# A gated SSD branch turned before its gate: from token-major to channel-major gating in a two-layer decoder trunk

## The chip, the cores and the metric

The kernel runs on one NeuronCore of a Trainium2 chip, as one launch. The metric is the device time of the launch in microseconds (us). Three runs of the kernel before took 1465.75, 1467.34 and 1467.36 us; the median is 1467.34 us. The profile was taken from a further execution.

## What is computed

The model is a trunk of two layers over 1024 prompt tokens, 16 meta tokens ahead of them and 8 sample tokens (one new token each, with a state of its own). Layer 0 is gated linear attention (GLA), layer 1 a Mamba-2 scan (SSD). Everything is fp32 in and out. What matters here is the end of layer 1's mixer (shapes: `l` tokens, 2048 channels in 4 groups of 512):

```python
S, y = segmented_scan(ssd_chunk_step, S0g, (x, dt, dt * A, Bm, Cm), seg_lens)
y = y + d_skip.astype(f32).reshape(SSD_GROUPS, SSD_HPG)[..., None] * x
y = y.reshape(bsz, l, SSD_DINNER) * jax.nn.silu(z)
yg = y.reshape(bsz, l, SSD_GROUPS, SSD_DINNER // SSD_GROUPS)
yg = yg * lax.rsqrt(jnp.mean(yg * yg, axis=-1, keepdims=True) + NORM_EPS)
y = yg.reshape(bsz, l, SSD_DINNER) * w_norm.astype(f32)
out = y.astype(h.dtype) @ w_out
```

So for each token and each group of 512 channels: the scan's output y is multiplied by a gate z, the mean of the squares of the product gives one factor per token, and the product goes through the output weights. The factor is applied after the output product.

## The kernel before, in words

**Tiling.** Tokens are cut into 9 steps: step s = 0 holds the 24 sample and meta tokens, steps 1 to 8 hold 128 prompt tokens each. Channels of a layer are cut into 4 units u. Steps 0 to 4 are group G = 0, steps 5 to 8 group G = 1. An event is one pair (u, s); layer 1 has 36, in the order G, u, s (`EVENTS`, line 54). Layer 1's outputs are handled in almost the same order (`OUTPUTS`, line 57), with step 0 of a unit behind its steps 1 to 4.

**Two kinds of work on TensorE.** The input projection ("pieces", line 1515) is cut into parts of 6 matmuls, with the weights and activations split into a high and a low fp32r half. The products with the output weights are at line 879: 24 matmuls of 512 columns for a step of 128 tokens. Between them stand the small fp32 matmuls of the scans.

**One order for all engines.** The class `Plan` makes one list of tasks. Every engine walks through this same list and issues what is its own, so each engine's instructions stand in the list's order and a wait at the head of an engine's queue holds up all that is behind it. A step of layer 1 is written by hand as a list of places (`ssd`, `first`, `step`, `close`, lines 231 to 247); a number beside a name says which event it serves (0: this one, 1: the next, -1: the one before). `("fill", x)` puts parts of the input projection there; x is a share, and the planner scales it so that a unit's pieces come out even. The pieces of the input projection run out in unit u = 2 of group 1: from there to the end the fills are empty. That stretch is the tail.

**An event of layer 1 before the change**, with its lines:

- scan: TensorE reads the state (2621), makes the state's update in the bank SU (2624) and the step's own part (2631). VectorE updates the state (2653, 2656) and sums the output y, 128 tokens on partitions x 512 channels, in SBUF (2645, 2660, 2664, 2668). The last of them counts up `y_summed`.
- gates: TensorE turns z, which was loaded with channels on partitions, into tokens on partitions, in bank SU (4 transposes, 2711; in the tail in another bank).
- norm: VectorE multiplies y by it (2725).
- inputs of the next event: TensorE turns x and B and multiplies B by C (2457 to 2459); ScalarE and VectorE prepare them (2466, 2485 to 2499).
- products of the event before: 24 matmuls (879); ScalarE (u = 0) or VectorE (line 2243, else) adds the two halves to the accumulator.
- turn: TensorE turns the gated y back to channels on partitions (4 transposes, 2741, bank SU). ScalarE copies it as the high half (2750), VectorE subtracts for the low half (2759). ScalarE squares the gated y and sums along the row (2734); GpSimd makes the mean and the root (2406, 2409).
- The next scan on TensorE waits until bank SU is read (`banks_free`, line 2563: `yt_lo`).

For step 0 the answers of the samples are turned as well (2695, with z at 2711) and added (2719). GpSimd also issues the loads and stores of the samples' states (2379, 2389). z comes from DRAM in the same task as the chunk of x, B, C, two events ahead (line 2333), on SP's queue; that queue also carries the weights (853, 857) and the stores of the pieces (1691).

Layer 0 has the same need and fills it in another way: its squares are made with channels on partitions and summed over partitions by matmuls against a column of ones (2164, 16 for a step), which ScalarE copies out (2176).

## Time and profile before

| | |
|---|---|
| runs shown | 1465.75, 1467.34, 1467.36 us; median 1467.34 us |
| profiled execution, its own time | 1462.42 us |
| its span | 1460.4 us |
| TensorE busy | 1399.5 us (96%) |
| VectorE busy | 1146.5 us (79%) |
| ScalarE busy | 832.8 us (57%) |
| GpSimd busy | 231.9 us (16%) |
| TensorE clock granted, mean | 0.991 of full speed |

PE is TensorE, PEld its weight loads, DVE VectorE, ACT ScalarE, POOL GpSimd, SPq SyncE's queue. Matmuls are pipelined: the duration of one includes its drain, so several in a row are closer together than they are long. Layer 1's events run from about 680 us to the end.

### The profile page before, as it was taken

The numbers are of one execution on the slowest core, as the hardware profiler recorded it, in microseconds if no ns is written. First come the engines' busy times: TensorE is split into PE (matmuls) and PEld (weight loads), VectorE is DVE, ScalarE is ACT, GpSimd is POOL, SyncE is SP. The second block draws the span as 40 slices with busy tenths as digits, with TensorE's granted clock in tenths as the row PEclk, the third lists the DMA queues.
The fourth block names the chain that finished last, engine by engine and source line by source line (L and its number), as shares of the span: only waits on it lengthen the run. The fifth ranks groups of instructions, "written<-read, shape, count | busy, mean of one in ns | idle before, by whom it ended". The sixth has DMA issues, their size and how long they took to land. (4 is left out here: it accounts for less than half of the span.)

```text
span 1460.4 us, 32342 instructions
## 1 busy us (share of the span) xinstructions
PE 1399.5 (96%) x12082; PEld 1173.2 (80%) x12082; DVE 1146.5 (79%) x2495; ACT 832.8 (57%) x1877; POOL 231.9 (16%) x429
## 2 busy tenths in 40 slices
PE   6999998999999899998999999989999999999987
PEld 6999897778888789997978888867777777777765
DVE  5566678676878987889796998986889688588786
ACT  5755645485556555556666664654656365555553
POOL 6010201011322100121211220120012110000003
PEclk9999999999999999998999999999999999999999
DMA  7485747266585435376844844852675674554463
GB/s 214 141 254 156 213 116 237 85 195 178 136 253 156 132 120 166 101 187 192 259 137 157 252 129 139 235 150 64 202 231 146 192 198 121 176 166 150 135 195 66
DMA packets 284454, 245.83 MB, mean 168 GB/s; under 512 B 33240, under 2 KB 251452, under 8 KB 283628
## 3 DMA queue, kind: packets, MB, share of 16 engines
q1 hardware_dynamic: 274204, 209.36, 48.2%
q0 software_dynamic: 10096, 34.41, 8.8%
q8 instruction: 97, 1.59, 0.4%
q14 instruction: 57, 0.47, 0.1%
HBM read 183.02 MB, written 65.00 MB: 170 GB/s over the span
## 5 line engine op out<-in xcount | busy, mean ns | idle before, releaser
L1515 PE MATMUL bank<-h,w 128*128 128x268 f32 (+1 forms) x4752 | 829.6, 328 | 7.6 <-ACT w L894 3.1
L1515 PEld LDWEIGHTS bank<-h,w 128*128 128x128 f32 x4752 | 694.8, 190 | 84.3 <-issue 11.2
L910 DVE TENSOR_TENSOR w<-w_raw,w 128x1024 fp32r<-128x1024 f32 x132 | 160.9, 1219 | 38.3 <-ACT w L894 38.1
L879 PE MATMUL bank<-s_w_out,s_yt_hi 128*128 128x512 f32 (+2 forms) x544 | 168.1, 398 | 1.7 <-DVE s_ys L2668 1.0
L894 ACT ACTIVATE w<-w_raw 128x1024 fp32r<-128x1024 f32 x132 | 138.8, 1052 | 11.2 <-DMA w_raw<-in_ssd_w_in_dram 5.9
L1593 DVE SCALAR_TENSOR_TENSOR conv<-before_conv,cw,conv 128x260 f32<-128x260 f32 (+2 forms) x216 | 125.2, 580 | 4.3
L879 PEld LDWEIGHTS bank<-s_w_out,s_yt_hi 128*128 128x128 f32 (+2 forms) x544 | 95.9, 180 | 28.1 <-issue 2.1
L879 PE MATMUL bank<-s_w_out,s_yt_lo 128*128 128x512 f32 x240 | 94.7, 395 | 0.0
L879 PE MATMUL bank<-g_w_out,g_ot_hi 128*128 128x512 f32 (+2 forms) x288 | 92.8, 410 | 0.3 <-DVE g_ot_lo L2186 0.3
L2431 ACT ACTIVATE s_decay<-s_decay,t_ac 128x128 f32<-128x128 f32 (+1 forms) x288 | 85.4, 379 | 1.2
L2750 ACT ACTIVATE s_yt_hi<-bank 128x512 fp32r<-128x512 f32 (+1 forms) x36 | 20.1, 558 | 115.3 <-PE bank L2741 115.1
L1561 ACT ACTIVATE conv<-bank,cw 128x268 f32<-128x268 f32 (+1 forms) x72 | 45.9, 637 | 67.8 <-PE bank L1515 51.9
L2406 POOL TENSOR_SCALAR s_ymean<-s_ysum 128x1 f32<-128x1 f32 (+1 forms) x36 | 16.4, 456 | 361.8 <-ACT squares L2734 361.7
L2389 POOL DMA_DIRECT2D out_dram<-s_sample_state x32 | 25.1, 785 | 302.6 <-DVE s_sample_state L2543 302.6
L1665 DVE SCALAR_TENSOR_TENSOR stage<-stage,conv 128x268 f32<-128x268 f32 (+1 forms) x72 | 37.3, 518 | 37.9 <-ACT stage L1622 37.7
L879 PEld LDWEIGHTS bank<-g_w_out,g_ot_hi 128*128 128x128 f32 (+2 forms) x288 | 50.0, 183 | 12.4 <-DVE g_ot_lo L2186 0.5
L2631 PEld LDWEIGHTS bank<-s_xdt,s_decay 128*32 128x32 f32 (+1 forms) x2112 | 33.7, 109 | 27.3 <-issue 27.3
L1553 ACT ACTIVATE conv<-bank 128x268 f32<-128x268 f32 (+1 forms) x72 | 32.8, 455 | 39.8 <-PE bank L1515 39.5
L2243 DVE SCALAR_TENSOR_TENSOR y_acc<-bank,s_yrstd,y_acc 128x512 f32<-128x512 f32 (+1 forms) x54 | 39.2, 744 | 19.5 <-PE bank L879 19.4
L1862 POOL TENSOR_SCALAR g_omean<-g_osum 128x1 f32<-128x1 f32 (+1 forms) x36 | 14.3, 397 | 251.2 <-ACT g_osum L2176 250.5
L879 PEld LDWEIGHTS bank<-s_w_out,s_yt_lo 128*128 128x128 f32 x240 | 45.2, 188 | 10.6
L1076 ACT ACTIVATE squares<-y_acc 128x512 f32<-128x512 f32 (+1 forms) x72 | 45.3, 629 | 14.0 <-DMA y_acc<-in_x_prompt_dram 5.3
(261 smaller groups left out, 2414.4 us busy)
## 6 DMA issues: line engine op xcount, KB each, us to landing
w_raw<-in_ssd_w_in_dram SPq DMA_DIRECT2D x80, 512.0 KB, 4.2
w_raw<-in_gla_w_in_dram SPq DMA_DIRECT2D x48, 512.0 KB, 4.6
s_decay<-kept_acd SPq DMA_DIRECT2D x32, 512.0 KB, 6.4
w_raw<-in_ssd_w_out_dram SPq DMA_DIRECT2D x30, 512.0 KB, 4.3
s_chunk<-kept_sq SPq DMA_DIRECT2D x32, 384.0 KB, 4.8
kept_sq<-stage SPq DMA_DIRECT2D x80, 134.0 KB, 4.4
g_chunk<-kept_gq SPq DMA_DIRECT2D x32, 320.0 KB, 4.3
kept_sq<-stage SPq DMA_DIRECT2D x40, 256.0 KB, 4.8
```

What stands on the lines that cost most here:

```text
L879: last = pe.matmul(bank[0:r, :], yt[a][:, k, 0:r], wo[:, b, 512 * half:512 * half + 512], start=(k + a + b == 0), stop=(k == tiles - 1 and ...
L894: act.activation(self.part(i, 0), self.raw(i), ACT.Copy).then_inc(self.w_hi, 1)
L910: dve.tensor_tensor(self.part(i, 1), self.raw(i), hi, ALU.subtract).then_inc(self.w_lo, 1)
L1076: act.activation(m["junk"][0:n, :], m["y"][0:n, s, 512 * half:512 * half + 512], ACT.Square, accum_out=m["stats"][0:n, half, j:j + 1]).the ...
L1515: last = pe.matmul(bank[:, 0:n], w[:, p.tile % 2, a, k, :], h[:, b, k, c:c + n], start=(i == 0), stop=(i == len(terms) - 1))
L1553: act.activation(self.work(i)[:, 0:n], bank[:, 0:n], ACT.Tanh, scale=0.5).then_inc(self.tanhed, 1)
L1561: act.activation(self.work(i)[:, 0:n], bank[:, 0:n], ACT.Identity, scale=m["cw"][:, 3, a:a + 1], bias=m["cw"][:, 4, a:a + 1])
L1593: return dve.scalar_tensor_tensor(out=u[:, off:n], in0=x[:, k:k + w], scalar=cw[:, k, a:a + 1], in1=u[:, off:n], op0=ALU.mult, op1=ALU.add)
L1665: dve.scalar_tensor_tensor(out=self.slot(i)[:, 0:n], in0=self.slot(i)[:, 0:n], scalar=1.0, in1=self.work(i)[:, 0:n], op0=ALU.add, op1=ALU. ...
L2243: return dve.scalar_tensor_tensor(out=y, in0=bank, scalar=rstd, in1=y, op0=ALU.mult, op1=ALU.add)
L2431: last = act.activation(L[0:n, r, :], L[0:n, r, :], ACT.Relu, scale=-1.0, bias=ac[0:n, s, h:h + 1])
L2631: last = pe.matmul(self.own(u, s)[rows, r * HD:(r + 1) * HD], G[0:n, r, rows], t["xdt"][0:n, r * HD:(r + 1) * HD], start=True, stop=True)
```

## The change

Layer 1's scan output y (not yet gated) is turned to channels on partitions, right behind the inputs of the next event, and gated there: z is used as it was loaded. z is not turned any more, nor are the samples' answers. VectorE multiplies the turned y (bank) by z (SBUF) into a new SBUF tile `og`, [128, 4, 128]. ScalarE copies `og` as the high half (task `highs`), VectorE subtracts for the low half. ScalarE then squares `og` in place, behind the subtraction, without a row sum. GpSimd folds the four blocks of squares into one with two additions (128x256, then 128x128). At the end of the event's step (task `sums`, just before the last fill) TensorE sums over partitions with a column of ones, 4 matmuls into SU; ScalarE copies the sums out, and GpSimd makes the root from them. The next scan waits for that copy. For step 0, y is turned and copied to SBUF by VectorE (task `first_out`). z's load is a task of its own (`z_in`), behind the products.

```diff
-        ssd = [("decay", 1), ("scan", 0), ("fill", 0.5), ("lows",),
-               ("weight", 3, 1), ("fill", 0.5), ("gates", 0), ("load", 2), ("lows",), ("fill", 0.3), ("norm", 0),
-               ("inputs", 1), ("products_late", -1), ("weight", 0, 0), ("fill", 0.5), ("lows",), ("fill", 0.5),
-               ("products_first", -1), ("turn", 0), ("square", 0), ("weight", 1, 0), ("r_add", -2), ("r_in", -1),
-               ("fill", 0.3), ("lows",), ("weight", 2, 0), ("fill", 0.3), ("r_square", -1), ("r_out", -2), ("fill", 0.3)]
+               ("weight", 3, 1), ("fill", 0.5), ("load", 2), ("lows",), ("fill", 0.3),
+               ("inputs", 1), ("turn", 0), ("norm", 0), ("products_late", -1), ("z_in", 2), ("weight", 0, 0), ("fill", 0.5), ("lows",), ("fill", 0.5),
+               ("products_first", -1), ("highs", 0), ("square", 0), ("weight", 1, 0), ("r_add", -2), ("r_in", -1),
+               ("fill", 0.3), ("lows",), ("weight", 2, 0), ("fill", 0.3), ("r_square", -1), ("r_out", -2), ("sums", 0),
+               ("fill", 0.3)]
...
-        step = [("decay", 1), ("scan", 0), ("fill", 0.6), ("lows",), ("weight", 1), ("fill", 0.5), ("gates", 0),
-                ("load", 2), ("lows",), ("fill", 0.4), ("norm", 0), ("inputs", 1), ("products", -1),
-                ("weight", 2), ("fill", 0.4), ("lows",), ("spread", 0), ("fill", 0.1), ("sample", 0), ("fill", 0.6), ("turn", 0), ("square", 0), ("weight", 3),
+        step = [("decay", 1), ("scan", 0), ("fill", 0.6), ("lows",), ("weight", 1), ("fill", 0.5),
+                ("load", 2), ("lows",), ("fill", 0.4), ("inputs", 1), ("turn", 0), ("norm", 0), ("products", -1), ("z_in", 2),
+                ("weight", 2), ("fill", 0.4), ("lows",), ("spread", 0), ("fill", 0.1), ("sample", 0), ("fill", 0.6), ("highs", 0), ("square", 0), ("weight", 3),
                 ("r_add", -2), ("r_in", -1), ("fill", 0.3), ("lows",), ("sample", 1), ("fill", 0.4),
-                ("r_square", -1), ("r_out", -2), ("fill", 0.3)]
+                ("r_square", -1), ("r_out", -2), ("sums", 0), ("fill", 0.3)]
...
+    def load_z(self, sp, u, s):
+        t, d, (c, n) = self.t, self.d, step_cols(s)
+        q = self.z_count(u, s)
+        if q >= 2:
+            sp.wait_ge(self.gated, oev(*[x for x in EVENTS if x[1]][q - 2]) + 1)
...
+    def pool_fold(self, pool, u, s):
+
+        o, og, n = oev(u, s), self.t["og"], step_cols(s)[1]
+        pool.wait_ge(self.rows.squared, self.rows.squares[("square", 1, u, s)])
+        pool.tensor_tensor(og[:, 0:2, 0:n], og[:, 0:2, 0:n], og[:, 2:4, 0:n], ALU.add).then_inc(self.folds, 1)
+        pool.wait_ge(self.folds, 2 * o + 1)
+        pool.tensor_tensor(og[:, 0, 0:n], og[:, 0, 0:n], og[:, 1, 0:n], ALU.add).then_inc(self.folds, 1)
...
+        self.turn_read(pe, e)
+        if issued["sums"]:
+            pe.wait_ge(self.sums_kept, issued["sums"])
...
+    def turn_outputs(self, pe, u, s):
+        n = step_cols(s)[1]
+        pe.wait_ge(self.y_summed, ev(u, s) + 1)
+        for j in range(4):
+            last = pe.transpose(self.y_bank(u, s)[:, j * n:(j + 1) * n], self.t["y"][0:n, j * P:(j + 1) * P],
+                                self.m["ident"][0:n, 0:n])
+        last.then_inc(self.y_turned, 1)
...
+        dve.tensor_tensor(t["og"][:, :, 0:n], y, z, ALU.mult).then_inc(self.gated, 1)
...
+    def act_highs(self, act, u, s):
         t, o, n = self.t, oev(u, s), step_cols(s)[1]
         act.wait_ge(self.gated, o + 1)
+        if o:
+            act.wait_ge(self.out_done, 2 * o)
+        act.activation(t["ythi"][:, :, 0:n], t["og"][:, :, 0:n], ACT.Copy).then_inc(self.yt_hi, 1)
+
+    def dve_lows(self, dve, u, s):
+        t, o, n = self.t, oev(u, s), step_cols(s)[1]
+        dve.wait_ge(self.yt_hi, o + 1)
+        dve.tensor_tensor(self.low_part(s), t["og"][:, :, 0:n], t["ythi"][:, :, 0:n].bitcast(F32),
+                          ALU.subtract).then_inc(self.yt_lo, 1)
+
+    def act_square(self, act, u, s):
+
+        t, o, n = self.t, oev(u, s), step_cols(s)[1]
+        act.wait_ge(self.yt_lo, o + 1)
+        before = self.rows.squares[("square", 1, u, s)] - 1
+        act.wait_ge(self.rows.squared, before)
+        act.activation(t["og"][:, :, 0:n], t["og"][:, :, 0:n], ACT.Square).then_inc(self.rows.squared, 1)
+
+    def pe_sums(self, pe, u, s):
+
+        o, n = oev(u, s), step_cols(s)[1]
+        pe.wait_ge(self.folds, 2 * (o + 1))
+        for j in range(0, n, SUB):
+            k = min(SUB, n - j)
+            last = pe.matmul(self.SU[j:j + k, 0:1], self.t["og"][:, 0, j:j + k], self.m["ones"][:, 0:1], start=True, stop=True)
+        last.then_inc(self.summed, 1)
...
```

## Rows read from the trace of the kernel before

**Rows 1.** Busy time by stretch: us, PE, PEld, DVE, ACT, POOL, PEclk, DMA, GB/s

```profile
680.00:1160.00 480.00, 464.17 (x3696) 387.96 (x3685) 406.42 (x983) 281.76 (x710) 82.26 (x126) 0.99 0.59 175
1160.00:1388.00 228.00, 227.68 (x1631) 176.68 (x1630) 174.23 (x258) 123.21 (x263) 17.67 (x28) 1.00 0.54 160
1388.00:1460.40 72.40, 58.31 (x567) 43.54 (x565) 56.95 (x81) 34.66 (x92) 14.29 (x29) 0.95 0.48 131
```

**Rows 2.** Groups on PE by form: busy us, mean ns, idle before and its releasers

```profile
L2711 PE MATMUL bank<-ident,s_z 128*128 128x128 f32 x128 | 19.7, 276 | 4.4 <-DVE states L2656 4.2 <-DVE s_yt_lo L2759 0.2
L2164 PE MATMUL bank<-ones,g_o_squares 128*32 128x1 f32 x512 | 9.9, 174 | 0.0
L2711 PE MATMUL bank<-ident,s_z_first 128*24 128x128 f32 x16 | 2.4, 273 | 0.0
```

**Rows 3.** Timeline of PE in the tail: start, us, engine, line

```profile
1433.84 0.60 PE L2741 MATMUL bank<-ident,s_ys 128*128 128x128 f32 x4
...
1437.12 0.66 PE L2711 MATMUL bank<-ident,s_z 128*128 128x128 f32 x4
1437.53 0.72 PE L879 MATMUL bank<-w,s_yt_hi 128*128 128x512 f32 x2
...
1443.22 0.60 PE L2741 MATMUL bank<-ident,s_ys 128*128 128x128 f32 x4
...
1445.23 0.73 PE L879 MATMUL bank<-w,s_yt_hi 128*128 128x512 f32 x2 [0.98 <-DVE s_yt_lo L2759]
```

**Rows 4.** Timeline of DVE in the same stretch

```profile
1440.56 0.69 DVE L2668 TENSOR_TENSOR s_ys<-s_ys,s_xw 128x512 f32<-128x512 f32 x1
...
1443.42 0.75 DVE L2243 SCALAR_TENSOR_TENSOR y_acc<-bank,s_yrstd,y_acc 128x512 f32<-128x512 f32 x1 [0.79 <-PE bank L879]
1444.49 0.69 DVE L2759 TENSOR_TENSOR s_yt_lo<-bank,s_yt_hi 128x512 fp32r<-128x512 f32 x1 [0.32 <-ACT s_yt_hi L2750]
1445.10 1.28 DVE L1133 SCALAR_TENSOR_TENSOR y_acc<-y_acc,stats,norm_weight 128x1024 f32<-128x1024 f32 x1
```

**Rows 5.** Groups on ACT by form: squares, and layer 0's copy of sums

```profile
L2734 ACT ACTIVATE squares<-s_ys 128x512 f32<-128x512 f32 x32 | 19.9, 623 | 0.0
L2176 ACT ACTIVATE g_osum<-bank 128x1 f32<-128x1 f32 x32 | 5.4, 169 | 14.5 <-PE bank L2164 14.4
```

**Rows 6.** POOL's additions by source line (ns min/median/max), and the timeline of POOL

```profile
L1812 POOL TENSOR_TENSOR g_lmask<-g_lmask x1: 458/458/458, 25.9 to 25.9; 128x128 f32<-128x128 f32 x1
L1088 POOL TENSOR_TENSOR stats<-stats x36: 179/203/2591, 4.9 to 1452.7; 128x1 f32<-128x1 f32 x32, 24x1 f32<-24x1 f32 x4
...
1445.16 1.26 POOL L2406 TENSOR_SCALAR s_ymean<-s_ysum 128x1 f32<-128x1 f32 x1 [5.32 <-ACT squares L2734]
```

**Rows 7.** Timeline of PE and DVE around a turn in group 1

```profile
1222.64 0.60 PE L2741 MATMUL bank<-ident,s_ys 128*128 128x128 f32 x4
1222.99 4.42 PE L1515 MATMUL bank<-h,w 128*128 128x512 f32 x18
1227.25 1.02 PE L2621 MATMUL bank<-states,s_chunk 128*128 128x512 f32 x2
...
1223.26 0.69 DVE L1665 SCALAR_TENSOR_TENSOR stage<-stage,conv 128x512 f32<-128x512 f32 x1 [3.10 <-ACT stage L1622]
```

**Rows 8.** Timeline of PE and DVE around a turn in group 0

```profile
862.56 0.60 PE L2741 MATMUL bank<-ident,s_ys 128*128 128x128 f32 x4
862.92 2.47 PE L1515 MATMUL bank<-h,w 128*128 128x268 f32 x18
867.15 1.10 PE L2621 MATMUL bank<-states,s_chunk 128*128 128x512 f32 x2 [1.76 <-issue]
...
866.36 0.68 DVE L2759 TENSOR_TENSOR s_yt_lo<-bank,s_yt_hi 128x512 fp32r<-128x512 f32 x1
```

**Rows 9.** PE after a wait, and the stretch behind it

```profile
510.09 0.49 PE L2130 MATMUL bank<-g_attn,g_v_turned 128*128 128x128 f32 x2 [2.78 <-DVE g_attn L2044]
...
511.50:514.90 3.40, 3.40 (x9) 2.63 (x9) 3.37 (x5) 0.00 (x0) 0.00 (x0) 0.50 1.03 367
```

More of the change, by code:

```diff
@@ L200, in stage @@
             if 0 <= e < len(EVENTS):
-                outputs = L == 1 and (name.startswith("r_") or name in ("gates", "norm", "turn", "square", "products"))
+                outputs = L == 1 and (name.startswith("r_") or name in ("sums", "norm", "turn", "highs", "square", "products"))
                 u, s = (OUTPUTS if outputs else EVENTS)[e]
@@ L243, in skeleton @@
                 ("r_add", -2), ("r_in", -1), ("fill", 0.3), ("lows",), ("sample", 1), ("fill", 0.4),
-                ("r_square", -1), ("r_out", -2), ("fill", 0.3)]
-        close = [("gates", 0), ("fill", 0.4), ("lows",), ("norm", 0), ("products", -1), ("fill", 0.4), ("turn", 0),
+                ("r_square", -1), ("r_out", -2), ("sums", 0), ("fill", 0.3)]
+        close = [("fill", 0.4), ("lows",), ("norm", 0), ("products", -1), ("fill", 0.4), ("highs", 0),
                  ("square", 0), ("r_add", -2), ("r_in", -1), ("fill", 0.4), ("lows",), ("r_square", -1),
-                 ("r_out", -2), ("fill", 0.4)]
+                 ("r_out", -2), ("sums", 0), ("fill", 0.4)]
@@ L461, in fill_in @@
                     self.last_norms()
-                if task[0] in ("distance", "state", "attend", "scale", "values", "decay", "scan", "gates", "inputs",
-                               "products", "sample", "turn"):
+                if task[0] in ("distance", "state", "attend", "scale", "values", "decay", "scan", "sums", "norm", "inputs",
+                               "products", "sample", "turn", "first_out", "highs"):
                     self.drain_norm()
@@ L620, in _ @@
             elif name == "square" and at[0] == 1:
+                ssd.pool_fold(pool, *at[1:])
+            elif name == "sums":
                 ssd.root(pool, *at[1:])
@@ L657, in _ @@
                 layers[at[0]].act_square(act, *at[1:])
-            elif name == "turn":
-                layers[at[0]].act_turn(act, *at[1:])
+            elif name == "turn" and at[0] == 0:
+                gla.act_turn(act, *at[1:])
+            elif name == "highs":
+                ssd.act_highs(act, *at[1:])
+            elif name == "sums":
+                ssd.act_sums(act, *at[1:])
             elif name == "products" and at[1] == 0:
@@ L706, in _ @@
                 ssd.dve_meta(dve, *at)
-            elif name == "turn":
-                layers[at[0]].dve_turn(dve, *at[1:])
+            elif name == "first_out":
+                ssd.dve_first(dve, *at)
+            elif name == "turn" and at[0] == 0:
+                gla.dve_turn(dve, *at[1:])
+            elif name == "highs":
+                ssd.dve_lows(dve, *at[1:])
             elif name == "products" and at[1] > 0:
@@ L2269, in __init__ @@
                                                          for x in ("ck_in", "acb_in", "z_in", "back"))
-        self.issued, count = {}, dict.fromkeys(("inputs", "spread", "scan", "gates0", "turn", "products"), 0)
+        self.issued, count = {}, dict.fromkeys(("inputs", "spread", "scan", "sums", "products"), 0)
         for name, *at in W.plan.order:
@@ L2274, in __init__ @@
                 self.issued[(name, u, s)] = dict(count)
-                if name == "gates" and s == 0:
-                    count["gates0"] += 1
-                elif name in count and not (name == "turn" and self.late(u, s)):
+                if name in count:
                     count[name] += 1
-            elif name == "meta":
+            elif name in ("meta", "first_out"):
                 self.issued[(name, *at)] = dict(count)
@@ L2401, in root @@
         q = slice(o % 4, o % 4 + 1)
-        pool.wait_ge(self.rows.squared, self.rows.squares[("square", 1, u, s)])
+        pool.wait_ge(self.sums_kept, o + 1)
         if o >= 4:
@@ L2577, in last_banks_free @@
         if (u, s) == self.LATE[0]:
-            pe.wait_ge(self.yt_lo, self.issued[("scan", u, s)]["turn"])
+            self.turn_read(pe, e)
+        pe.wait_ge(self.sums_kept, self.issued[("scan", u, s)]["sums"])
         pe.wait_ge(self.y_summed, e)
@@ new lines, in dve_first, with pe_turn @@
+    def dve_first(self, dve, u):
+        dve.wait_ge(self.y_turned, ev(u, 0) + 1)
+        if u:
+            dve.wait_ge(self.gated, oev(u - 1, 0) + 1)
+        dve.tensor_copy(self.t["y0"][:, :, :], self.y_of(u, 0)).then_inc(self.first_kept, 1)
+    def pe_turn(self, pe, u, s):
+        if self.late(u, s):
+            pe.wait_ge(self.gated, oev(u, s))
+        elif self.issued[("turn", u, s)]["sums"]:
+            pe.wait_ge(self.sums_kept, self.issued[("turn", u, s)]["sums"])
+        self.turn_outputs(pe, u, s)
@@ L2731, in act_square @@
             act.wait_ge(self.rooted, o - 3)
-        before = self.rows.squares[("square", 1, u, s)] - 1
-        act.wait_ge(self.rows.squared, before)
-        act.activation(self.m["junk"][0:n, :], self.outputs(s)[0:n, :], ACT.Square,
-                       accum_out=t["ysum"][0:n, o % 4:o % 4 + 1]).then_inc(self.rows.squared, 1)
-    def pe_turn(self, pe, u, s):
-        o, n = oev(u, s), step_cols(s)[1]
-        pe.wait_ge(self.gated, o + 1)
-        for j in range(4):
-            last = pe.transpose(self.y_bank(u, s)[:, j * n:(j + 1) * n], self.outputs(s)[0:n, j * P:(j + 1) * P],
-                                self.m["ident"][0:n, 0:n])
-        last.then_inc(self.y_turned, 1)
```

141 lines of the change are left out of this document (59 added, 82 removed).

## The prediction

> **What bounds the kernel now.** I read the page's busy times first, then the busy times by stretch, the groups on TensorE, and last the timelines around single events. By stretch [rows 1], TensorE is the bound of layer 1's body and nearly without gaps: 464.2 of 480 us in group 0, 227.7 of 228 us in group 1 up to the tail. VectorE is close behind it in group 0 (406.4 of 480, 85%) and not in group 1 (76%). In the tail, from 1388 us on, TensorE has 58.3 of 72.4 us and VectorE 57.0: no projection is left to put into a wait, so what counts there is the chain from one event to the next. The question is therefore double: how much TensorE work goes, and whether the new chain (highs, lows, squares, two folds, sums) is done when TensorE comes to it. TensorE takes its queue in order, so a wait at `sums` stops everything.
>
> **TensorE's work.** Removed: 32 sets of four z transposes. They are busy 19.7 us [rows 2], 0.62 us a set with the drain that overlaps the next work; from a set's start to the next work it is 0.41 us (1437.12 to 1437.53, [rows 3]). I take 0.41: 13.1 us, bounds 13.1 and 19.7. For step 0, z and the samples' answers are turned by equal sets: busy 2.4 us for one kind [rows 2], so 4.8 for both, 3.2 without drains if they shrink in the same ratio 0.41/0.62. Together -16.3 us. The y transposes only move. Added: 36 sets of 4 sum matmuls. Layer 0's 16 of the same form are busy 9.9/32 = 0.31 us a step [rows 2], so a set of 4 is between a quarter of that and all of it, 0.08 to 0.31. A first matmul in another mode costs its own lead, so I take 0.2: +7.2 us (2.9 to 11.2). The waits ahead of the z transposes, 4.4 us [rows 2], go too, though their releaser is VectorE's state update and `turn` now waits for the end of the same chain (y summed): I take -4 with 0 and -4.4 as ends. Sum of this part: -13 us, ends -24 and -2.
>
> **VectorE, ScalarE, SP at nothing.** VectorE gates 128x512 as before, one operand in a bank; the lows change their operand from bank to SBUF. Sums that copy and addition for step 0 save on VectorE are under 1 us a unit and beside other work. The square loses its accumulator read; the copy of sums, 0.17 us in layer 0 [rows 5], takes its place. z's load is issued behind the products and waits for a gating two z loads back, with the weights' loads behind it on SP; the load has most of an event to land (events are 19 to 24 us apart in the body, 9 to 12 in the tail). Cover gone, it would cost the delay once per event; I put 0, end +5 in all.
>
> **The new chain.** From the start of VectorE's subtraction: 0.69 (row 2759 in [rows 4]), ScalarE's square 0.62 [rows 5], the two folds, and 0.06 for handing over at four places (the subtraction ends at 1444.49 + 0.69 = 1445.18 and TensorE starts at 1445.23 [rows 3, 4]). The highs run on ScalarE beside VectorE's adds and cost nothing while they are shorter than these. GpSimd's fold is shown by one addition of 128x128, 0.46 us, and by additions of one column, 0.20 [rows 6]. So 2 ns a column over 0.2: 0.72 for 256 columns, 0.46 for 128, 1.18 together; from below it is two additions at 0.20, from above two at 1.26, the longest mean step in those rows. Chain: 0.69 + 0.62 + 1.18 + 0.24 = 2.7 us from the subtraction's start to TensorE's sums (1.95 to 4.1).
>
> **The tail.** Before, the step between two turns is 1443.22 - 1433.84 = 9.4 us there [rows 3], and about 11 on the mean from 1388 us on. The order of an event is now scan, inputs, turn, products of the event before, sums, with nothing between. The subtraction stands on VectorE behind the adds of those products: the last add starts 0.2 us after the last matmuls and takes 0.75 (1443.42, [rows 4]), then the chain of 2.7. Then sums 0.2 and ScalarE's copy 0.17, with two handings over, before the next scan may start. So from the products' end: 0.2 + 0.75 + 2.7 + 0.2 + 0.17 + 0.1 = 4.1 us of idle TensorE in place of nothing. Besides, `turn` has moved ahead of the products and waits for y summed: that comes at 1440.56 + 0.69 = 1441.25, 4.1 us behind the z set's start. With the subtraction long done VectorE is less late than here, so I take 0.7 of wait. Against these stand the z set, 0.41, and the gaps that the tail has already (0.98 in [rows 3]; together some 5 us over the stretch). For the five events whose sums stand before a scan: 5 x (4.1 + 0.7 - 0.41) = 22; for the last event the products wait through sums as well, 4.0 in place of 2.0 (1443.22 to 1445.23, [rows 3]): +2; minus 5 for the old gaps: +19 us. Ends: +12 with the short folds, +26 with long ones. This is outside the -13 above except for the z sets, 2.4 us, which I leave as margin.
>
> **Group 1 before the tail.** At 1222.64 TensorE is at the place where `highs` will stand; VectorE is busy with a piece until 1223.95 [rows 7], so the chain ends at +1.3 + 2.7 = +4.0 us. TensorE has 18 matmuls of 512 columns until the scan [rows 7], 12 of them before `sums` (fills of 0.6 of 0.9): +2.8. It waits 1.2 us. I read the ten events 1172 to 1388 in the same way: one or two have the chain ready, the others lack 1.2 to 3; the sum is 15.7 us. I take 13, since some of it is lag that a wait elsewhere lets VectorE catch up; ends 6 and 20.
>
> **Group 0.** Here VectorE is later. At 862.56 the subtraction starts 3.8 us behind TensorE's place [rows 8], chain end +6.5; TensorE has 18 matmuls of 268 columns (2.5 us) and then already waited 1.76 us until that subtraction. The twenty events sum to 47 us in this static reading. But at 85% much of VectorE's lag is backlog, a wait gives it back, and waits like the 1.76 are counted twice. I take half, 23 us, ends 10 and 47.
>
> **The clock.** After a wait of 2.78 us (with a smaller one just before) the granted clock stood at 0.50, the lower level, for 3.4 us [rows 9]; that costs half of it, 1.7 us. In other places a gap of this size left the clock alone. Waits of 3 to 4 us in the tail make this likelier: +3 us, ends 0 and 20.
>
> **Sum.** -13 + 19 + 13 + 23 + 3 = +45; the execution profiled took 1462.42 (span 1460.4 and 2.0 around it), 4.9 below the median of the runs. I round to +43 for what is counted twice between the parts, and put it on the median: 1467.3 + 43 = **1510 us**. This measurement can tell about 0.2% (3 us) from no change.
>
> **Rivals.**
> 1. *The port* (chance 0.17). GpSimd's step of one column took 1.26 us at 1445.16, where its median is near 0.2, while VectorE ran a 1.28 us operation with both inputs in SBUF from 1445.10 [rows 4, 6]. If each event's folds meet such a one, they end 0.8 us later on the mean: 36 x 0.8 = 29 us more, about 1539. Against it: most of VectorE's work reads a bank. The Trainium skill ("SBUF — State Buffer", Who interferes with whom) says that a VectorE instruction with two SBUF inputs and a GpSimd instruction that reads SBUF exclude each other; by that rule the trace agrees with its 1.26 us.
> 2. *Only the tail pays* (0.12). If VectorE's lag in the body is all backlog, the chain is ready at `sums` there; then -13 + 19 + 0 to 6, 1473 to 1479.
> 3. *Faster: the chain fits* (0.09). The mechanism is the fold's length: with additions of 0.2 us the chain is 1.95, the tail costs 12, the body's waits vanish as in rival 2 and the transposes give their upper bound: -24 + 12 = -12, 1455. It decides if the folds together take under 0.5 us and the body's waits sum to under 10. For it: TensorE is at 97 to 100% in the body [rows 1], so removed work counts fully. Against: [rows 7, 8].
> 4. *The removed work gives nothing*, because VectorE bounds group 0. It is part of the forecast: it takes group 0's 16 sets out of the -13, +7 us at most.
>
> **How the numbers follow.** Forecast 0.62, port 0.17, only the tail 0.12, faster 0.09. The forecast's own ends, if all go one way, are -24 + 12 + 6 + 10 = +4 and -2 + 26 + 20 + 47 + 20 = +111; not all will, and I take +15 to +70 for it. Rival 2 lies at the low side and half of rival 1 at the high side, so 1474 to 1542 for 8 in 10. Slower takes the forecast, the port and nearly all of rival 2; faster has 0.08; 0.05 is left for no change.
>
> **What would show it.** In the profile after: PE idle at the sums' line, with POOL's fold as releaser, 3 to 5 us at each of the last five events and 1 to 2 on the mean in the body; the four-transpose sets down from 72 to 36; folds of about 0.7 and 0.5 us; step length in the tail 13 to 15 us. I am wrong if the waits at `sums` sum to under 20 us, if the sums come before VectorE's adds in the tail, or if the folds are far from 1.2 us.

## The result and the profile after

The kernel after took 1590.35 us (median of four runs, 1586.02 to 1594.51), against 1466.55 us before (four runs, 1463.88 to 1467.36): ratio 1.086, with a 95% interval of 1.083 to 1.089. It is slower, as predicted, but by 124 us where 43 were forecast; 1590 lies above the range of 1474 to 1542.

**Where the time is.** The page of the kernel after (its busy times, and the granted clock in 40 slices):

```profile
span 1591.1 us, 32631 instructions
PE 1440.7 (91%) x12186; PEld 1191.0 (75%) x12186; DVE 1151.3 (72%) x2499; ACT 838.8 (53%) x1877; POOL 279.8 (18%) x501
PEclk9999999999999999998999999999999999999888
```

The span grew by 130.7 us (1460.4 before). TensorE's idle time grew from 60.9 (1460.4 - 1399.5) to 150.4 us (1591.1 - 1440.7), +89.5. Its busy time grew by 41.2, although the z transposes are gone. So there are two losses to explain, and the second is not added work. By stretch, cut at the same scans of 128 tokens in both kernels (us; "lower" is TensorE's busy time at the lower clock, read from the clock records of the two traces):

| stretch | length before, after | more idle | more lower |
|---|---|---|---|
| to the first such scan | 677.7, 686.4 (+8.7) | 0.8 | 11.0 |
| the rest of group 0 | 477.9, 535.1 (+57.2) | 42.2 | 49.7 |
| group 1 up to the tail | 221.5, 247.7 (+26.2) | 20.1 | 15.5 |
| the tail | 83.3, 121.9 (+38.6) | 26.3 | 27.2 |

The first row is mostly layer 0, whose tasks the change leaves as they were: its last sum matmul starts at 641.6 us in place of 635.2. No run tells why; in the profiles of the other kernels below layer 0 ends 0.2 to 6.3 us later than in that of before. So some 6 us of the 130.7 are not explained by anything that follows.

**The idle time.** The waits of TensorE after, by waiting line and releaser, for group 0 (680 to 1220 us), for group 1 up to the tail (to 1478), and for the tail (us in total, times, longest):

```profile
PE bank L2788 <- POOL s_yt_gated L2423: 46.8, 18, 5.5
PE bank L2656 <- issue: 8.0, 5, 3.5
...
PE bank L2788 <- POOL s_yt_gated L2423: 15.1, 8, 2.8
PE bank L2656 <- issue: 5.4, 3, 3.0
...
PE bank L2788 <- POOL s_yt_gated L2423: 24.8, 6, 5.2
PE bank L2721 <- DVE s_ys L2701: 4.7, 5, 1.6
PE bank L2656 <- ACT s_ysum L2796: 2.4, 4, 0.6
```

L2788 is the new sum matmul: 86.7 us over 32 waits, with GpSimd's second fold as releaser. L2656 is the scan's first matmul (2621 before). Of its waits after, 8 with 13.4 us have no releaser in the view ("issue"); in each of them ScalarE's copy of the sums (L2796) ended 0.1 to 0.2 us before the matmul started, so it is the copy that they wait for. By stretch, with the columns of [rows 1]:

```profile
680.00:1220.00 540.00, 481.96 (x3725) 397.41 (x3723) 410.96 (x1003) 283.02 (x706) 106.00 (x162) 0.95 0.53 157
1220.00:1478.00 258.00, 237.53 (x1742) 179.36 (x1743) 177.48 (x260) 129.79 (x277) 32.97 (x54) 0.97 0.49 144
1478.00:1591.10 113.10, 72.65 (x601) 49.51 (x599) 59.72 (x84) 36.59 (x92) 21.38 (x41) 0.83 0.32 84
```

**The busy time.** The same work has become slower. Groups by form after (total us, mean ns):

```profile
L2656 PE MATMUL bank<-states,s_chunk 128*128 128x512 f32 x64 | 47.8, 840 | 15.9 <-issue 13.4 <-ACT s_ysum L2796 2.4
L2721 PE MATMUL bank<-ident,s_ys 128*128 128x128 f32 x128 | 19.6, 276 | 4.7 <-DVE s_ys L2701 4.7
L2788 PE MATMUL bank<-ones,s_yt_gated 128*32 128x1 f32 x256 | 8.2, 188 | 84.3 <-POOL s_yt_gated L2423 84.3
L2421 POOL TENSOR_TENSOR s_yt_gated<-s_yt_gated 128x256 f32<-128x256 f32 x32 | 27.0, 843 | 372.4 <-ACT s_yt_gated L2780 372.4
L2423 POOL TENSOR_TENSOR s_yt_gated<-s_yt_gated 128x128 f32<-128x128 f32 x32 | 18.1, 565 | 2.5
L2780 ACT ACTIVATE s_yt_gated<-s_yt_gated 128x512 f32<-128x512 f32 x32 | 20.2, 631 | 67.6 <-DVE s_yt_lo L2771 67.6
```

The sum matmuls cost 9.0 us (8.2 shown, and 0.8 for the short steps), close to the 7.2 forecast, and the turn 276 ns a matmul. But the scan's first matmul (two instructions), which stands right behind the waits, takes 840 ns an instruction in the mean, where the same view of before has 600:

```profile
L2621 PE MATMUL bank<-states,s_chunk 128*128 128x512 f32 x64 | 33.2, 600 | 7.7 <-issue 5.9 <-DVE s_yt_lo L2759 1.7
```

Why shows in windows laid over stretches that follow a wait:

```profile
998.80:1005.60 6.80, 6.22 (x78) 3.47 (x79) 5.50 (x18) 4.51 (x14) 2.91 (x5) 0.50 0.27 77
1538.10:1544.90 6.80, 4.79 (x44) 2.20 (x48) 1.41 (x3) 5.58 (x18) 2.84 (x7) 0.50 0.00 0
```

The granted clock there is 0.50, that is 1.2 of 2.4 GHz. The clock records of the trace hold 31 such stretches, 141.7 us within the span, and TensorE is busy in 123.1 of these; before there were 6 with 27.3 us, 19.6 of it busy. The scan's first matmul takes twice as long there (2.05 against 1.02 us), so I count half of the additional 103.5 us, 52 us, as lost to it. The check: -22.1 (z transposes, [rows 2]), -2.4 (the samples' answers, L2695, 16 transposes), +9.0 (sums), +52 gives +36.5, against +41.2 measured. About 4 us of the 52 fall into layer 0. The Trainium skill ("TensorE: Matmul & The Clock Gate", HAM oscillation) counts a loss in the same way, half of the throttled time, in a kernel that waits again and again for data; this trace agrees to within 5 us (36.5 and 41.2), with the idle part left out.

The clock does not follow the single wait exactly. After its start TensorE waits 28 times for more than 2 us. Behind 25 of these waits the clock was at 0.50 within 1.4 us of their end; after the others (2.06 us up to 1020.2, 2.98 up to 1351.9, 2.84 up to 1399.3) it stayed at 1.00.

**One event of the body**, TensorE, then VectorE, ScalarE and GpSimd (start, us, engine, line):

```profile
992.39 1.04 PE L1159 MATMUL bank<-ident,y_acc 128*128 128x128 f32 x8
998.93 0.28 PE L2788 MATMUL bank<-ones,s_yt_gated 128*32 128x1 f32 x8 [5.50 <-POOL s_yt_gated L2423]
999.66 2.05 PE L2656 MATMUL bank<-states,s_chunk 128*128 128x512 f32 x2 [0.45 <-issue]
...
996.19 0.68 DVE L2771 TENSOR_TENSOR s_yt_lo<-s_yt_gated,s_yt_hi 128x512 fp32r<-128x512 f32 x1
998.83 1.13 DVE L2567 SCALAR_TENSOR_TENSOR s_sample_state<-bank,s_x_columns,s_sample_state 128x128 f32<-128x128 f32 x4 [1.96 <-ACT s_sample_state L2556]
...
996.91 0.63 ACT L2780 ACTIVATE s_yt_gated<-s_yt_gated 128x512 f32<-128x512 f32 x1 [2.45 <-DVE s_yt_lo L2771]
997.44 1.26 ACT L2556 ACTIVATE s_sample_state<-s_sample_state,t_cols 128x128 f32<-128x128 f32 x4
...
997.62 0.72 POOL L2421 TENSOR_TENSOR s_yt_gated<-s_yt_gated 128x256 f32<-128x256 f32 x1 [1.02 <-ACT s_yt_gated L2780]
998.42 0.46 POOL L2423 TENSOR_TENSOR s_yt_gated<-s_yt_gated 128x128 f32<-128x128 f32 x1
```

Read from below: fold 998.42 + 0.46 = 998.88, and TensorE's sums at 998.93. From the subtraction's start (996.19) to the sums is 2.74 us, where 2.7 were forecast. But ScalarE stands still for 2.45 us ahead of the square (L2780), and the samples' scaling (L2556) is queued behind it; VectorE then stands still for 1.96 us until that scaling is done. Here the two engines wait for each other in turn, and the scan's matmuls (2.05 in place of 1.02 us) run at the lower clock.

**The tail.** TensorE after, from one `sums` to the next:

```profile
1539.51 0.29 PE L2788 MATMUL bank<-ones,s_yt_gated 128*32 128x1 f32 x8 [3.51 <-POOL s_yt_gated L2423]
1540.39 2.04 PE L2656 MATMUL bank<-states,s_chunk 128*128 128x512 f32 x2 [0.60 <-ACT s_ysum L2796]
1542.23 1.92 PE L2659 MATMUL bank<-s_xw,s_b_turned 128*128 128x512 f32 x2
1544.08 1.47 PE L2666 MATMUL bank<-s_xdt,s_decay 128*32 128x64 f32 x64
...
1547.19 0.63 PE L2721 MATMUL bank<-ident,s_ys 128*128 128x128 f32 x4 [0.72 <-DVE s_ys L2701]
1557.22 0.24 PE L2788 MATMUL bank<-ones,s_yt_gated 128*32 128x1 f32 x8 [3.82 <-POOL s_yt_gated L2423]
```

The step is 1557.22 - 1539.51 = 17.7 us, forecast 13 to 15, 9.4 before [rows 3]. The waits are those of the prediction, 3.8 us at the sums, 0.7 at the turn, 0.6 for ScalarE's copy. The scan's part takes 5.1 us (1540.39 to 1545.48, where the inputs begin) in place of 2.8 before (1434.28 to 1437.12): that is the clock, 0.50 in 1538.1 to 1544.9. The row of its start before:

```profile
1434.28 1.02 PE L2621 MATMUL bank<-states,s_chunk 128*128 128x512 f32 x2
```

### The profile page after: what moved, and what is told of

Read it like the earlier page. It is cut to its first block and busy times, and to the rows that moved or that the text cites. A ratio compares the mean times of both kernels' runs of the same rounds, so it can differ in the third digit from the quotient of the medians.

```text
span 1591.1 us, 32631 instructions
## 1 busy us (share of the span) xinstructions
PE 1440.7 (91%) x12186; PEld 1191.0 (75%) x12186; DVE 1151.3 (72%) x2499; ACT 838.8 (53%) x1877; POOL 279.8 (18%) x501
## 5 line engine op out<-in xcount | busy, mean ns | idle before, releaser
L1533 PEld LDWEIGHTS bank<-h,w 128*128 128x128 f32 x4752 | 706.6, 193 | 85.2 <-issue 10.2
L897 PEld LDWEIGHTS bank<-s_w_out,s_yt_hi 128*128 128x128 f32 (+2 forms) x544 | 96.1, 180 | 24.5
L2421 POOL TENSOR_TENSOR s_yt_gated<-s_yt_gated 128x256 f32<-128x256 f32 (+1 forms) x36 | 28.8, 801 | 412.2 <-ACT s_yt_gated L2780 412.2
L1579 ACT ACTIVATE conv<-bank,cw 128x268 f32<-128x268 f32 (+1 forms) x72 | 46.0, 639 | 86.7 <-PE bank L1533 78.9
L2788 PE MATMUL bank<-ones,s_yt_gated 128*32 128x1 f32 (+1 forms) x264 | 9.1, 187 | 86.7 <-POOL s_yt_gated L2423 86.7
L2457 ACT ACTIVATE s_decay<-s_decay,t_ac 128x128 f32<-128x128 f32 (+1 forms) x288 | 85.3, 379 | 1.2
L2788 PEld LDWEIGHTS bank<-ones,s_yt_gated 128*32 128x32 f32 (+1 forms) x264 | 6.0, 117 | 99.3 <-POOL s_yt_gated L2423 99.0
L2766 ACT ACTIVATE s_yt_hi<-s_yt_gated 128x512 fp32r<-128x512 f32 (+1 forms) x36 | 21.2, 589 | 95.9 <-PE bank L897 89.6
L2666 PEld LDWEIGHTS bank<-s_xdt,s_decay 128*32 128x32 f32 (+1 forms) x2112 | 38.5, 122 | 36.3 <-issue 36.3
L2656 PE MATMUL bank<-states,s_chunk 128*128 128x512 f32 x64 | 47.8, 840 | 15.9 <-issue 13.4
L1880 POOL TENSOR_SCALAR g_omean<-g_osum 128x1 f32<-128x1 f32 (+1 forms) x36 | 15.1, 418 | 255.2 <-ACT g_osum L2194 254.5
```

The lines of the kernel that those rows point to most:

```text
L897: last = pe.matmul(bank[0:r, :], yt[a][:, k, 0:r], wo[:, b, 512 * half:512 * half + 512], start=(k + a + b == 0), stop=(k == tiles - 1 and ...
L1533: last = pe.matmul(bank[:, 0:n], w[:, p.tile % 2, a, k, :], h[:, b, k, c:c + n], start=(i == 0), stop=(i == len(terms) - 1))
L1579: act.activation(self.work(i)[:, 0:n], bank[:, 0:n], ACT.Identity, scale=m["cw"][:, 3, a:a + 1], bias=m["cw"][:, 4, a:a + 1])
L2421: pool.tensor_tensor(og[:, 0:2, 0:n], og[:, 0:2, 0:n], og[:, 2:4, 0:n], ALU.add).then_inc(self.folds, 1)
L2457: last = act.activation(L[0:n, r, :], L[0:n, r, :], ACT.Relu, scale=-1.0, bias=ac[0:n, s, h:h + 1])
L2656: pe.matmul(self.from_state(u, s)[0:n, :], x[:, 5, :], self.S[:, u % 2, :], start=True, stop=True).then_inc(self.inter, 1)
```

## The experiments

Theory from here on: TensorE's wait for the chain VectorE's subtraction, ScalarE's square, folds, sums, copy costs twice, as idle time and as work at the lower clock behind it. Rivals: the folds on GpSimd (and the port) are the price; ScalarE's blocked square is; or something of the change that has nothing to do with the sums. All ratios are to the kernel before, run on the same chip at the same time (medians 1462.6 to 1465.2 us in the experiments). Idle and lower come from one profiled execution each. Idle is TensorE's, "lower" is the busy time of TensorE at the granted clock 0.50 from the trace's clock records.

| run | us | ratio, 95% | idle | lower |
|---|---|---|---|---|
| before | 1466.55 | 1 | 60.9 | 19.6 |
| after | 1590.35 | 1.083 to 1.089 | 150.4 | 123.1 |
| no folds | 1559.55 | 1.063 to 1.068 | 123.5 | 94.6 |
| filler | 1607.53 | 1.096 to 1.101 | 60.4 | 22.9 |
| half the filler | 1568.66 | 1.069 to 1.075 | 85.8 | 43.4 |
| sums ahead | 1517.63 | 1.035 to 1.039 | 105.2 | 66.5 |
| sums ahead, no folds | 1521.20 | 1.036 to 1.041 | 98.1 | 64.3 |
| sums behind | 1526.07 | 1.040 to 1.045 | 112.9 | 78.2 |
| own squares | 1546.92 | 1.053 to 1.060 | 126.4 | 78.7 |
| squares first | 1527.50 | 1.039 to 1.046 | 107.5 | 61.4 |
| squares first, no folds | 1502.52 | 1.021 to 1.029 | 90.6 | 52.7 |
| sums of a constant | 1550.68 | 1.057 to 1.062 | 124.3 | 95.8 |
| no sums | 1492.73 | 1.015 to 1.021 | 94.0 | 72.2 |
| no sums, squares first | 1481.59 | 1.008 to 1.013 | 85.3 | 56.0 |

**Without the folds** (GpSimd makes none; TensorE sums the four blocks of squares itself, 16 matmuls).

```diff
-        pool.tensor_tensor(og[:, 0:2, 0:n], og[:, 0:2, 0:n], og[:, 2:4, 0:n], ALU.add).then_inc(self.folds, 1)
-        pool.tensor_tensor(og[:, 0, 0:n], og[:, 0, 0:n], og[:, 1, 0:n], ALU.add).then_inc(self.folds, 1)
...
-        pe.wait_ge(self.folds, 2 * (o + 1))
+        pe.wait_ge(self.rows.squared, self.rows.squares[("square", 1, u, s)])
```

> The changed kernel, but GpSimd folds nothing: TensorE sums all four blocks of squares (16 matmuls an event in place of 4). Theory (the wait at sums, as long as its chain, plus the clock it brings down): the two folds, 0.84 + 0.57 us and one handing over, leave each event's chain, so the 32 waits shrink by 1.5 us each (-48 us), 16 matmuls cost 5 us more, and with fewer long waits the time at half clock falls from 144 us to some 80 (-30 us): about 1520 us. Rival (VectorE or the order of the transposes sets the pace, the wait at sums only shows it): under 15 us less. Rival (port): VectorE's busy time falls too, by several us.

1559.55 us, 31 less than after. The waits of this kernel on TensorE:

```profile
PE bank L2785 <- ACT s_yt_gated L2776: 39.5, 22, 4.2
PE bank L2652 <- issue: 27.7, 12, 4.9
```

So the folds are worth a quarter of the loss, net of the 12 matmuls that replace them in each event. That is less than the 1520 us expected, and more than the first rival's 15 us. With them gone the sums wait for ScalarE's square, and the next scan (L2652) waits more. The port cannot be much: VectorE's busy time is 1148.4 us here and 1151.3 with the folds.

**Filler in the wait.** Ahead of the wait for the folds TensorE multiplies the identity by itself, into the bank that the sums overwrite; nobody reads it. First 16 products for each set of sums (36 in the last events), then half of that:

```diff
+        self.turn_read(pe, ev(*(u, 4) if s == 0 else (u, s)) + 1)
+        pe.wait_ge(self.sums_kept, o)
+        for j in range(36 if ev(u, s) >= ev(U - 2, 7) else 16):
+            pe.matmul(self.SU[:, 128 * (j % 4):128 * (j % 4) + 128], self.m["ident"][:, :], self.m["ident"][:, :], start=True, stop=True)
         pe.wait_ge(self.folds, 2 * (o + 1))
```

> The changed kernel with matmuls that nobody reads ahead of each sums wait, 16 of 128 columns (1.8 us) in the body and 36 (3.9 us) in the last events, into the bank that is free there. The extra work computes nothing. Theory that the clock is a cost of its own: the chain is unchanged and mostly covers the matmuls, so idle time turns into busy time, the time at the lower level falls from 144 us to under 60, and the kernel gets faster by 25 to 50 us although it does more: 1545 to 1565. Rival (the lower clock costs nothing, since it falls into waits): no faster, 1590 to 1605.

> The changed kernel with half the idle matmuls of the earlier run (8 in the body, 18 in the last events; there 16 and 36 took longer than the waits that they were to fill, so that run told of their length too). Their length is now about 1.8 and 3.9 us, most of it inside the waits. They compute nothing that is read. Theory that the lower clock costs time: time at it from 144 us to under 60, kernel 15 to 40 us faster than the changed one, 1550 to 1575. Rival: no faster, 1590 or more.

The full filler overran the waits (each fp32 product is two instructions): 1607.5 us, above both ranges that were expected, so it decides nothing about the sum; but the additional time at the lower clock is gone, 22.9 us against 19.6 before the change. The half filler does: TensorE is busy for 1479.0 us in place of 1440.7, it does 38 us more, and the kernel is 22 us faster than after. The page's first line and clock of this kernel:

```profile
PE 1479.0 (95%) x12882; PEld 1249.2 (80%) x12882; DVE 1150.3 (74%) x2499; ACT 838.0 (54%) x1877; POOL 274.1 (18%) x501
PEclk9999999999999899989999999999999999999999
```

Half of 123.1 - 43.4 is 40 us of time at the lower clock avoided. A second reading comes near it: the filler's 696 instructions are busy 83.5 us, and without them TensorE would be busy 1395.5 us, 45 less than in the kernel after. That the clock costs time of its own, and not only the wait ahead of it, is shown by this pair.

**The sums one place later.** In the next event, behind its scan, either ahead of its inputs or behind them; the wait for the folds then has the scan and the fills around it as cover, and no scan waits for a copy that was just made.

```diff
-                ("load", 2), ("lows",), ("fill", 0.4), ("inputs", 1), ("turn", 0), ("norm", 0), ("products", -1), ("z_in", 2),
+                ("load", 2), ("lows",), ("fill", 0.4), ("sums", -1), ("inputs", 1), ("turn", 0), ("norm", 0), ("products", -1), ("z_in", 2),
...
-                ("r_square", -1), ("r_out", -2), ("sums", 0), ("fill", 0.3)]
+                ("r_square", -1), ("r_out", -2), ("fill", 0.3)]
```

> The changed kernel with sums taken off the step's end and put into the next event, just ahead of its inputs; all else as changed. Theory: the chain has the scan and two fills more to end in; nothing waits in the body, about 1 us an event in the tail; the change then shows what its removed transposes are worth: 1455 to 1475 us. Rival (y turned ahead of the products waits for y summed, or VectorE bounds): waits move to the turn or the scan and the time stays above 1500.

> As the run with sums ahead of the next inputs, but just behind them: the turn that follows needs the same bank and waits for ScalarE's copy of the sums. Theory: 0.3 to 0.4 us more wait for 36 events, less about 0.7 us in the tail's six: 5 to 12 us slower than sums ahead. Rival (the bank is not waited for): the same within 2 us.

1517.63 us, 73 less than after, though not the 1455 to 1475 expected. In place of 86.7 us for GpSimd TensorE waits in this kernel (L2794 sums, L2725 turn):

```profile
PE bank L2794 <- DVE states L2693: 21.8, 7, 5.8
PE bank L2725 <- ACT s_ysum L2802: 18.4, 9, 4.3
...
PE bank L2794 <- POOL s_yt_gated L2427: 7.0, 4, 3.7
PE bank L2725 <- DVE s_ys L2705: 6.3, 8, 1.8
```

The sums share bank SU with the state's update, and must let VectorE read that first. Behind the inputs it is 8 us slower (1526.1): the copy of the sums is then the turn's wait, 25.5 us.

**The same without folds** (both edits, sums ahead).

> The sums moved into the next event ahead of its inputs, as in an earlier run (1517.6 us), and besides no folds: 16 sum matmuls straight on the squares. Theory (there the folds are done in time, since the sums come after the next scan): 12 more matmuls of 0.05 to 0.1 us on 36 sets, +20 to +30 us at most, against 7 us of waits for GpSimd: 1515 to 1540 us. Rival (the folds were still late there and their square's rows held VectorE's gating): 1495 to 1510 us.

1521.2 us (1515.7 to 1523.3), against 1517.6: no difference to be told. TensorE's busy time is 5.4 us longer (1415.8 against 1410.4), its idle time 7.1 shorter. Where the sums come late enough, the folds cost no more than the 12 matmuls that replace them. Most of their price in the change is a matter of place.

**Squares out of VectorE's reach.** In the change the square is made in place, so it must wait for the subtraction that reads the same tile. Here the squares go to a tile of their own (the scan output's, free from the turn to the next scan's sum; VectorE's first write there waits for the sums now). In the second kernel the square also stands ahead of the highs, which wait for the products of the event before; in the third the folds are gone too.

```diff
-        act.wait_ge(self.yt_lo, o + 1)
+        act.wait_ge(self.gated, o + 1)
...
-        act.activation(t["og"][:, :, 0:n], t["og"][:, :, 0:n], ACT.Square).then_inc(self.rows.squared, 1)
+        act.activation(t["ysq"][:, :, 0:n], t["og"][:, :, 0:n], ACT.Square).then_inc(self.rows.squared, 1)
```

> The changed kernel, but the squares go into a tile of their own (the scan's output tile, free in that time), so ScalarE squares right behind the highs and does not wait for VectorE's subtraction. Theory: VectorE's lag (its place is 1 to 4 us behind TensorE's) and its 0.69 us leave the chain, and ScalarE no longer stands still for it (67.6 us of waits): the waits at sums fall from 87 to 25 to 40 us, with the clock's share 1500 to 1530. Rival (the folds and GpSimd's queue hold the chain): under 20 us less. Rival (only the clock matters): waits fall and the time with it, but not by more than the waits.

> As the run with squares in a tile of their own, and ScalarE squares ahead of the highs, so that in the tail squares and folds run beside the products of the event before. Theory: the chain is 0.6 us shorter in the body and off the path in the tail (4 us an event for six events); waits at sums under 15 us; 1465 to 1490. Rival (in the tail it is the turn's wait for y summed and ScalarE's copy): waits move there, 1495 or more.

> As squares first, and TensorE sums the four blocks itself, no folds on GpSimd. Theory: where the chain is already done the folds cost nothing, so 12 more matmuls an event cost 3 to 6 us and the remaining waits give that back: within 6 us of squares first. Rival (folds still on the path): over 10 us faster.

Own squares 1546.9 (-43 against after), first 1527.5 (-63), first without folds 1502.5 (-88). The first two gained less than the theory expected (1500 to 1530, 1465 to 1490); the second landed in its rival's range, where waits move to the turn and to the copy. The wait at the sums falls from 86.7 to 54.2 and 30.0 us, then to nothing, and the wait ahead of the scan stays and grows, from 15.8 to 34.0 us in the third. That the third is 25 us below the second says that the folds were still on the path, which the rival there had. Squares first, with folds, then without (L2792 sums, L2657 and L2653 scan):

```profile
PE bank L2792 <- POOL s_ys L2424: 30.0, 15, 4.6
PE bank L2657 <- issue: 19.9, 10, 4.0
```

```profile
PE bank L2653 <- issue: 27.3, 13, 4.1
...
PE bank L2653 <- ACT s_ysum L2797: 6.7, 4, 2.2
```

This is the best of the kernels that compute everything, and still 2.5% slower than before.

**Cutting the chain.** Three kernels in which the row factors are those of a constant. First the sum matmuls read the identity tile and wait for no fold, only for their bank and the copy before; squares, folds and the copy stay. Then there are no sum matmuls, no wait for the copy, and ScalarE copies a column of ones. Last, this and the squares in their own tile ahead of the highs.

```diff
-        pe.wait_ge(self.folds, 2 * (o + 1))
...
-            last = pe.matmul(self.SU[j:j + k, 0:1], self.t["og"][:, 0, j:j + k], self.m["ones"][:, 0:1], start=True, stop=True)
+            last = pe.matmul(self.SU[j:j + k, 0:1], self.m["ident"][:, j:j + k], self.m["ones"][:, 0:1], start=True, stop=True)
```

> The change, but the four sum matmuls read the constant identity tile in place of the folded squares and do not wait for GpSimd's folds (squares and folds are still made; nothing reads them, so the row factors are those of a constant). ScalarE's copy of the sums still stands behind its square, and the next scan still waits for that copy. Theory (the price lies in TensorE's in-order wait for a chain through VectorE's subtraction and ScalarE's square, the folds being only its last part): most of the wait moves from the sums to the next scan, one fill of 0.3 and 1.4 us of folds later; 1525 to 1555 us, the wait ahead of the scan up from 16 to 45 to 70 us. Rival (the folds and GpSimd's semaphore hand-over are the price): under 1500 us. An earlier run without folds gave 1559.6, which speaks against the rival.

> The change without the sum matmuls: TensorE makes no sums and waits for none, the next scan waits for no copy, ScalarE copies a column of ones in the place of the sums (so the row factors are constant). Squares and folds are still made. Theory (all that the change costs hangs on TensorE's waits for this chain and on the clock behind them): what is left is the removed z transposes (-16), no sum matmuls, and the wait for y summed ahead of the moved turn (up to 12 us): 1450 to 1475 us, gaps on TensorE 50 to 65 us, time at the lower clock 30 to 50 us. Rival (the moved turn, the gating or ScalarE's blocked square cost by themselves, through later highs and later lows ahead of the products): 1490 to 1520 us.

> As the run without sum matmuls and without any wait for them (1492.7 us, 27 above the kernel before, though 16 us of transposes are gone and nothing is added on TensorE); and besides the squares go to a tile of their own, stand ahead of the highs and wait for the gated product alone. ScalarE copies a column of ones in the place of the sums. What is left of the change on TensorE is the z transposes gone and the turn moved ahead of the products. Theory (the rest of the loss is ScalarE standing still in the square for VectorE's subtraction, which makes the next event's copies, and so its scan, late): 1455 to 1475 us, ScalarE's 71 us of waiting at the square down under 25, the waits ahead of the inputs and of the turn (22.8 and 17.2 us) halved. Rival (the rest is the moved turn, which waits for y summed): 1485 to 1500 us, the wait at the turn still 15 us or more.

Sums of a constant, 1550.7 us: the wait of 86.7 us vanishes at the sums, and the one ahead of the scan rises from 15.8 to 69.3 us:

```profile
PE bank L2656 <- issue: 53.9, 17, 5.8
PE bank L2656 <- ACT s_ysum L2798: 15.4, 4, 5.1
```

In each of these 21 waits the copy had ended 0.1 to 0.4 us before the matmul started. Only 40 us are won, because the copy stands on ScalarE behind the square, which waits 68.8 us for VectorE. So the folds and GpSimd are the smaller part of it. Without sums, 1492.7 us: 98 of the 124 us hang on the sums. The other 26 do not, and here the theory missed (1450 to 1475 expected); the rival's 1490 to 1520 held. With the square in its own tile and ahead of the highs as well, 1481.6 us: that gives 11 of these, and 15 to 17 stay (17 against the kernel before on its own chip, 1464.4). This lies between the two ranges that were expected (1455 to 1475, rival 1485 to 1500). ScalarE is not free in it: it still waits 51.1 us at the square, now for the gated product. The waits of this last kernel (L2720 turn, L2482 inputs of the next event, L2777 ScalarE's square):

```profile
PE bank L2720 <- DVE s_ys L2700: 17.4, 13, 4.0
PE bank L2482 <- issue: 11.0, 8, 3.1
...
PE bank L2482 <- DVE s_ys L2677: 6.6, 2, 4.4
...
ACT s_ys L2777 <- DVE s_yt_gated L2754: 51.1, 15, 6.3
```

The turn in its new place waits 17.4 us for y summed, the inputs 17.6 us (1.4 before, in the tail). Each of the ten waits of the inputs ended 0.1 us behind VectorE's first step of y (L2677), also where the view says "issue"; VectorE never stood idle ahead of that step, so it is VectorE's own queue that was late. A sum with numbers of this kernel, over the stretch behind layer 0: 17.4 + 17.6 - 1.4, less the 4.2 at the z transposes [rows 2], less 24.5 of removed transposes, plus 15.8 for the clock (41.0 against 9.4 us lower, halved), is +20.7; that stretch is 18.0 us longer. The other 6.4 of the 24.4 us by which its span (1484.8) exceeds that of before lie in layer 0, which ends later there too. The sum is rough: the waits overstate the additional idle time (22.8) by 6.6 us, and the other terms understate the busy time (-4.8) by 3.9. That the turn waits because of its new place follows from whom it waits for; why VectorE is later for the inputs stays open, and a kernel with the turn put back was not run.

## Why the prediction was wrong, and where it was right

**Right: direction, mechanism, price of one event.** TensorE idles at the sums' line with GpSimd's fold as releaser. Folds of 0.73 and 0.46 us (medians; means 0.84 and 0.57) against 0.72 and 0.46 taken; chain 2.74 in the event shown against 2.7; sums 9.0 against 7.2 us in all; tail waits of 3.5 to 5.2 us against 3 to 5. The tail's part, +19 with +26 as end: TensorE's listed waits there are 31.9 us (24.8 + 4.7 + 2.4) against 4.8 before, +27, less 2.4 for the z sets: 25. Near the upper end, so the term was a little small. The tail as a whole grew by 38.6 us; what is above the waits is the clock, 13.6 us (half of 27.2), which the prediction kept apart.

**Wrong, step "Group 0" (and "Group 1 before the tail"): the discount for backlog.** The static reading gave 47 and 15.7 us; I took 23 and 13, on the ground that a wait lets VectorE catch up and that some waits are counted twice. Measured at the sums: 46.8 and 15.1. So the undiscounted reading was right in the sum, and the discount of 24 us in group 0 was the error; the single readings are not on record, so how well they agree event by event is not shown, and some of the closeness can be luck. The likely reason, argued from one event and the runs below, is that the step held VectorE's lag to be its own queue. ScalarE stands still 67.6 us ahead of the square for the subtraction, and what VectorE needs next is queued behind it, as at 996 us: there a wait on TensorE gave nothing back. The own-tile runs show what VectorE's place in the chain is worth: with VectorE out of it the waits at the sums fell from 86.7 to 54.2 us, and with the square ahead of the highs as well to 30.0.

**Wrong, step "The clock": +3 us with 20 as the upper end.** It was sized from one stretch [rows 9] and a few waits of the tail. It is 52 us: 31 stretches at the lower clock in place of 6, most of the new ones behind waits of 2 to 5.5 us all through layer 1. This is the largest missing term, and the half filler, which wins 22 us by doing more, shows that it is a cost of its own. The misses together lie outside what the prediction allowed for: even all upper ends of the forecast together, its clock end of 20 us among them, give 1578 us.

**Not priced: ScalarE's copy ahead of the scan.** It was priced in the tail (0.17 and two handings over, 0.6 measured) and not in the body. TensorE waited there 15.8 us ahead of the scan (13.4 + 2.4), against 7.6 before (5.9 + 1.7); when the sums no longer waited, it was up to 69.3 us.

**Half right: the turn's wait of 0.7.** In the kernel after it is 4.7/5 = 0.9 us. But this was small only because the sums held TensorE up long enough: without sums it is 17.2 us (17.4 in the last kernel).

**The sum with measured terms:** transposes and sums -15.5, idle time +89.5, clock +52: +126, for a span that is 130.7 longer. The transposes stand in this sum with their busy time, 24.5 us, where the prediction took 16.3 without the overlapped drains; no run separates the two.

**The rivals.** *The port*: 1539 was the closest number, for the wrong reason. The folds' means lie above their medians by 0.11 us each (843 and 565 ns), so 8 us for 72 folds, not 29, though 15 of the 32 wide folds took 0.91 to 1.04 us. The case that it was built on is there: a fold of 1.04 us that began at 1555.59, while VectorE had run its 1.28 us operation from 1554.77. *Only the tail pays*: falls with 61.9 us of waits at the sums in the body. *Faster*: falls; even with no sums at all the change is 1 to 2% slower. *The removed work gives nothing* was meant for group 0 alone; in the kernels without sums it looks as if it held for the whole, since the 24.5 us reappear as waits of the turn and of the inputs.

## What to carry to other kernels

When an in-order engine is given a wait, read the lag of its releasers at each place and add it up as it stands; discount it only if the trace shows that the releaser itself waits for nobody. This rests on one case. Where TensorE was 96% busy, price additional idle time at about one and a half times its length (1.45 to 1.79 here), for the clock behind it: in the kernel after 89.5 us of it brought 52 us of clock loss, and in the ten changed kernels without filler, worked out in the same way from the table, 24 to 66 us of it brought 0.45 to 0.79 of its length. Operations in place tie two readers together: here the square in place made ScalarE wait for VectorE, and cost 43 of 124 us; and a reduction whose result is not needed at once belongs behind the next independent piece of work, not in front of it (73 us here).

## What the runs showed of the hardware that was not expected

- TensorE is busy 91% of the span after and never waits longer than 5.5 us in layer 1, and still 141.7 us of the span were granted at 1.2 GHz. The scan's first matmul (two instructions of 512 columns) takes 2.05 us there and 1.02 us at 2.4 GHz.
- 348 products with no use (TensorE 38 us busier) made the kernel 22 us faster.
- Of 28 waits of TensorE over 2 us, 25 were followed by the lower clock and three (2.06, 2.98 and 2.84 us) were not.
